# Moving the split activations by 32 bytes in SBUF, from 64 to 96 bytes off the weights modulo 128

## What is computed

```python
# first block
h = rmsnorm(x, norm1_g);  hp = h @ w_in           # 1024 -> 512 + 512 + 768 + 24 + 2048
y_ssm = s5_mixer(hp[..., :o1], ...)               # state-space mixer, ends in a 512x512 gate
y_nsa = nsa_mixer(hp[..., o1:o2], ...)            # sparse attention
merged = gate0 * (y_ssm @ w_proj_ssm) + gate1 * (y_nsa @ w_proj_nsa)
x = x + merged @ w_out
x = x + jnp.square(jax.nn.relu(rmsnorm(x) @ w_up)) @ w_down           # 1024 -> 4096 -> 1024
# second block, layers 0 (retention) and 1 (latent attention)
for l in range(2):
    x = x + 0.5 * rms_norm(swiglu(rms_norm(x), w_gu[l, 0], w_down[l, 0]))   # 1024 -> 2 x 2816 -> 1024
    tok, qm = retention_mixer(...) if l == 0 else mla_mixer(...)
    x = x + rms_norm(concat([tok, memory_attention(qm, mem_n, w_kv[l])]) @ w_o[l])
    x = x + 0.5 * rms_norm(swiglu(rms_norm(x), w_gu[l, 1], w_down[l, 1]))
```

## Time and profile before

| | us |
|---|---|
| median of 3 runs (1472.91 to 1474.15) | 1473.9 |
| span of the profiled execution | 1470.6 |
| TensorE matmul busy in it | 1401.7 |
| TensorE weight load busy in it | 1358.3 |
| VectorE busy | 922.4 |
| ScalarE busy | 732.0 |
| GpSimd busy | 192.7 |

### The profile page before, as it was taken

The page is one execution under the profiler, slowest core; times in us unless marked ns, Lnnn a source line. Parts: engine busy times, 40 slices in busy tenths (PEclk is TensorE's granted clock), DMA queues, the critical chain, the costliest instruction groups (busy, mean ns, idle before and its releaser), DMA issues.

```text
span 1470.6 us, 28247 instructions
## 1 busy us (share of the span) xinstructions
PE 1401.7 (95%) x11538; PEld 1358.3 (92%) x11538; DVE 922.4 (63%) x1368; ACT 732.0 (50%) x1205; POOL 192.7 (13%) x210
## 2 busy tenths in 40 slices
PE   5899899999999999999998999999999989899998
PEld 5878799999999999998898999999999987899998
DVE  7998786666535665556765665556564467565644
ACT  7712755544435454455446454455444364554443
POOL 0465000022000111013101111011110010111100
PEclk9899899999999999999999999999999989999999
DMA  9223324455554555544342555544555341345551
GB/s 372 105 103 116 127 86 174 159 204 185 194 185 160 177 195 191 195 173 155 135 144 99 190 197 189 198 172 172 188 198 199 146 170 58 109 178 195 192 200 58
DMA packets 36815, 244.33 MB, mean 166 GB/s; under 512 B 4208, under 2 KB 5360, under 8 KB 8816
## 3 DMA queue, kind: packets, MB, share of 16 engines
q1 hardware_dynamic: 34992, 238.17, 44.7%
q10 hardware_dynamic: 1728, 4.81, 0.9%
HBM read 241.67 MB, written 1.05 MB: 165 GB/s over the span
## 4 chain that ended last, share of the span: by engine, by line
PE 81%; DVE 9%; ACT 5%; issue 2%; POOL 2%; DMA 1%; SPq 0%; DVEq 0%; ACTq 0%; POOLq 0%
PE ps L1891 49%; PE ps L1931 26%; DVE wlo L1083 3%; PE ps L2114 1%; PE ps L2140 1%; ACT whi L592 1%; DVE alo L1478 1%; PE ps L2130 1%; DMA xtok<-in_xt 1%; POOL pr L1809 1%; POOL pr L1808 1%; PE ps L2019 1%; ACT junk L829 1%; DVE yr L1456 0%; ACT pP L782 0%
## 5 line engine op out<-in xcount | busy, mean ns | idle before, releaser
L1083 DVE TENSOR_TENSOR wlo<-raw,whi 128x1024 fp32r<-128x1024 f32 (+1 forms) x434 | 505.1, 1205 | 273.3 <-ACT whi L592 273.2
L1891 PE MATMUL ps<-ahi,whi 128*128 128x256 f32 x2112 | 599.5, 284 | 32.1 <-DVE wlo L1083 18.0
L592 ACT ACTIVATE whi<-raw 128x1024 fp32r<-128x1024 f32 (+1 forms) x434 | 427.2, 1032 | 368.8 <-PE ps L1931 188.1
L1891 PE MATMUL ps<-alo,whi 128*128 128x256 f32 x2112 | 595.4, 282 | 0.0
L1891 PE MATMUL ps<-ahi,wlo 128*128 128x256 f32 x2112 | 594.0, 281 | 0.0
L1891 PEld LDWEIGHTS ps<-ahi,whi 128*128 128x128 f32 x2112 | 403.1, 191 | 38.2 <-issue 23.5
L1891 PEld LDWEIGHTS ps<-alo,whi 128*128 128x128 f32 x2112 | 402.8, 191 | 0.7 <-issue 0.7
L1891 PEld LDWEIGHTS ps<-ahi,wlo 128*128 128x128 f32 x2112 | 401.9, 190 | 0.0
L1829 POOL TENSOR_TENSOR hlo<-fh,hhi 128x256 f32 (+3 forms) x104 | 86.1, 828 | 756.2 <-ACT hhi L899 545.5
L1538 DVE TENSOR_TENSOR fa<-ps,r 128x512 f32<-128x512 f32 x104 | 71.9, 692 | 171.1 <-PE ps L1891 170.9
L1931 PE MATMUL ps<-whi,hhi 128*128 128x256 f32 x960 | 149.1, 277 | 0.0
(11 more groups left out here) (350 smaller groups left out, 1362.9 us busy)
## 6 DMA issues: line engine op xcount, KB each, us to landing
raw<-in_w_gu SPq DMA_DIRECT2D x88, 1024.0 KB, 4.8
raw<-in_w_fd SPq DMA_DIRECT2D x44, 1024.0 KB, 4.8
raw<-in_w_up SPq DMA_DIRECT2D x16, 1024.0 KB, 4.8
raw<-in_w_dn SPq DMA_DIRECT2D x16, 1024.0 KB, 4.8
raw<-in_w_ret SPq DMA_DIRECT2D x13, 1024.0 KB, 4.8
raw<-in_w_mg SPq DMA_DIRECT2D x8, 1024.0 KB, 4.9
raw<-in_w_o SPq DMA_DIRECT2D x8, 1024.0 KB, 6.3
raw<-in_w_mem SPq DMA_DIRECT2D x4, 1024.0 KB, 4.7
```

Source lines behind the costliest of these rows:

```text
L592: nc.scalar.activation(whi[:, m % SPL, c], raw[:, n % RAW, c], ACT.Copy).then_inc(S("w_hi"), 1)
L1083: ins = tt(wlo[:, m % SPL, c], raw[:, n % RAW, c], whi[:, m % SPL, c].bitcast(F32), ALU.subtract)
L1891: ins = mm(dst, lhsT, rhs, start=k == 0 and p == 0, stop=k == kt - 1 and p == len(pairs) - 1)
```

## The change

Three lines in the layout, none in the work: the instructions of all five engines, their order and their waits are the same.

```diff
@@ -279,10 +279,12 @@
         at_warm = [base[0] + 32]
         half_q = sb("half_q", [P, 1])
         warm = sb("warm", [P, 1], where=at_warm)
+        base[0] += 32
         at_ahi = [base[0]]
         ahi = sb("ahi", [P, KT, T], F32R)
         at_alo = [base[0]]
         alo = sb("alo", [P, KT, T], F32R)
+        base[0] += -base[0] % 64
         st = sb("st", [P, TT, 8])
         at_yT = [base[0]]
         yT = sb("yT", [P, KT, T])
@@ -382,7 +384,7 @@
         end_nsa = w[0]
 
         w = [phase]
-        w[0] += (64 - w[0]) % 128
+        w[0] += (96 - w[0]) % 128
         hhi = sb("hhi", [P, FF1_T, T], F32R, where=w)
         hlo = sb("hlo", [P, FF1_T, T], F32R, where=w)
         fa = sb("fa", [P, 2, 2 * T], where=w)
```

## The result

| | before | after |
|---|---|---|
| median, us | 1473.9 (1472.91 to 1474.15) | 1499.4 (1492.97, 1499.41, 1499.73) |
| ratio, 95% interval | | 1.0153 (1.0128 to 1.0178) |
| profiled execution: span, us | 1470.6 | 1491.2 |
| granted clock, mean | 0.982 | 0.987 |

The kernel became 1.5% slower, 25.5 us in the medians. The profiled execution of after is its fastest run. Its granted clock is higher, too: (1 - 0.982) x 1470.6 = 26.5 us of full-speed time were lost to the lower level before, (1 - 0.987) x 1491.2 = 19.4 us after. So the difference of the spans, 20.6 us, would be about 27.7 at an equal clock. This is an estimate: it takes TensorE to be at work while the clock is low, and the mean clock is known to 0.0005 only, 0.7 us each.

What follows compares the result with a forecast made beforehand. Bound taken as TensorE's matmul intervals, 1401.7 of 1470.6 us busy. Terms 3.0 + 9.2 + 0.8 + 1.1 - 1.0 = +13.1 us gave span 1483.7, median 1487.0; forecast's own range 1479 to 1499, 8 in 10 1436 to 1512.

Steps and rivals of the forecast that it cites:

- Gate and up projections, "117.8 already, 0": Four gate and up projections, 1008 matmuls each: already at the 117.8 ns assumed for the new distances, so 0 us.
- Up projection +3.0: First feed-forward's up projection, 720 matmuls: 84.8 in place of 81.8 us, +3.0 us.
- Four later down projections +9.2: Four later down projections, 528 matmuls each: 62.2 in place of 59.9 us, +2.3 each, +9.2 us.
- First down projection 0: First feed-forward's down projection, 768 matmuls: already at 117.8 ns, so 0 us.
- Single units +1.1, layer 1's output projection +0.8: Five single units rising from 5.44 to 5.66 us, +1.1; layer 1's mixer output projection, 192 matmuls from 113.8 ns, +0.8.
- `mhi` pairs -1.0: 432 matmuls with `mhi`/`mlo` and the `y` pairs go from distance 0 to 64, from 120.0 to 117.8 ns: -1.0 us.
- Everything else 0: Residual transposes, half a microsecond at most, and other engines' writes starting at multiples of 32, covered by matmuls: 0 us.
- From span to median +3.3: Whole runs: their median lies 3.3 us above the profiled span, so 1483.7 becomes 1487.0 us.
- 96 parts the readers: Rival, main streams: distance 96 parts weight load and stream; 1427 us at 111.7 ns, or 1444 at 113.4; chance 0.22.
- The sign matters: Rival: units at 96 good, downs at 32 bad, 1466 us, chance 0.14; the other way round, +12, counted with forecast.
- 32 and 96 are worse than 0: Rival, units and down projections: 120.0 ns everywhere gives +33 us, 1507; 123 ns gives 1537; chance 0.15.
- Nothing that counts: Rival: halfway value is 116.7 ns, 1476 us, or the address does not matter, 1474 us; chance 0.15 together.

Runs made afterwards that it cites:

- weights_back: Against the change, weights raw, whi, wlo moved to 96 modulo 128, everything behind them back on multiples of 64, distances unchanged: 1495.9 us.
- ahi96: Half of the change: against the kernel before, only ahi/alo moved to 96; hhi shifted along, putting down projections at distance 64: 1501.6 us.
- d32: Against the kernel before, activations placed 32 bytes past the weights modulo 256 (units at 32, down projections at 224): 1487.2 us.
- both32: Against the kernel before, activations placed 32 past the weights modulo 128, in fact units at 160 and down projections at 96 modulo 256: 1490.6 us.
- d0: Against the kernel before, activations at the same address as the weights modulo 256 (units and down projections at 0): 1505.2 us.
- d192: Against the kernel before, ahi/alo and hhi/hlo moved by 128 bytes, so units at 192 and down projections at 64: 1461.7 us.
- wide: Addresses of the kernel before; matmuls in down stream 512 columns per weight load in place of 256: 1481.1 us.
- roots5: Layout of the kernel before; a short product formed twice ahead of the units that follow, so the long stream starts at another moment: 1476.3 us.
- d192_wide0: Against the kernel before, units at 192 and down projections at 0 with 512-column matmuls, three rounds: median 1454.6 us, ratio 0.9877.

## Why the prediction was right or wrong

The direction held, and so did the idea that the distance between the operands sets the interval. The form that the prediction gave this idea did not: the distance doesn't count modulo 128, and the interval at 96 isn't halfway between those at 0 and 64. +13.1 us was forecast, +25.5 measured, and two terms make most of the difference.

- **Gate and up projections, "117.8 already, 0":** This is the step that failed. They take 120.0 ns: +2.2 us each, +8.9 in all. The prediction called itself wrong above 1 ns per matmul, and they moved by 2.2. The median, 1499.4, lies just past the 1479 to 1499 of the forecast itself; the wider range, 1436 to 1512, held it because 1507 had been counted as a rival. Underneath was "halfway between distance 0 and distance 64, since 32 and 96 both lie halfway". weights_back and ahi96 show that 96 has the ceiling, as 0 has; d32 shows 116.7 to 117.8 at 32. The ceiling itself, 120.0 "with nothing to forbid more", was not passed in any stretch by more than 0.3 ns.
- **Up projection +3.0:** +4.8, by the same term.
- **Four later down projections +9.2:** +8.3. The value for -96 was nearly right, 117.4 ns for 117.8, by luck: it is 160 and not 32.
- **First down projection 0:** +0.7 us (118.7 ns). weights_back has 117.3 ns in the same place at the same distance, so this place has two values at one distance, too.
- **Single units +1.1, layer 1's output projection +0.8:** the five units moved by 0.3 us each as forecast, but those at 5.66 moved by 0.1 as well. The remainder, 27.7 less 22.7, about 5 us at an equal clock and not known to better than 1 or 2 us, must lie in these and the units between the stretches; it was not parted further.
- **`mhi` pairs -1.0:** 117.9 ns for the 117.8 forecast.
- **Everything else 0:** right. weights_back takes the writes of the other engines out; `alo` at the transitions kept its 2.43 us.
- **From span to median +3.3:** the profiled runs lie 1.7 to 1.9 us above their spans. The rest of the 3.3 was the difference between one run and the median.

**The rivals.** "96 parts the readers" is out: 96 has the longest interval. "The sign matters" is right as a mechanism (both32), in the form the prediction wrote as "the other way round": units at 120.0, and its +12 was too low, as the downs did not fall to 113.4. "32 and 96 are worse than 0" came nearest in size, 1507, and is half right: 96 has the 120.0 ns of 0, and -96 does not. "Nothing that counts" is out. The rule of the Trainium skill ("SBUF — State Buffer", section "SBUF: two separate sides") that TensorE's ports never wait on anyone doesn't bear the reading that an address can't matter to TensorE; whether a port waits, no run shows. d0 and d192 hold the same instructions at other addresses; a gate and up projection takes 120.94 us in one and 114.25 in the other.

**What stays open.** That the load of the next weights and the stream collide was only inferred. wide refuted its simplest form, and no run shows the collision. Why one distance has two forms, and what chooses between them, is open as well: wide and roots5 changed it in streams whose instructions and addresses are as before, d192 shows both forms among four equal projections, and none of it was foretold. So part of what d192_wide0 wins could be lost by an edit elsewhere. A second profile of one kernel would show whether the form repeats. The distances of 16, 48 and 112 weren't tried, nor units with 512 columns.

One small reading of the prediction was off: the 128-column row gives (1.84 - 0.28) / 14 = 111.4 ns and not 112. No term of the forecast uses it.

## What to carry to other kernels

When TensorE is busy all the time and waits for nothing, divide a long stretch of the chain by its matmuls: if one shape shows several intervals, the placement of its operands may be a knob, here 1505 against 1462 us by placement alone (single runs of d0 and d192). Tabulate the distance moving minus stationary modulo 256 for each pair, and don't interpolate between two measured distances; a run with one tensor moved is cheap, and a price found for 256 columns doesn't hold for 512. Judge such a change by stretches at full clock, as whole runs of one kernel spread over 15 us.

## What the runs showed of the hardware that was not expected

- The interval of a matmul with 128 x 128 float32r weights and 256 columns depends on the distance between its operands, given here modulo 256. From the long gate and up and later down projections: 0: 120.0 ns, even; 32: 116.7 or 117.8; 64: 113.4 or 117.8; 80: 118.3 or 120.0; 96: 120.0; 128: 118.7; 160: 117.3; 176: 118.8; 192: 113.3 or 117.8; 224: 118.4.
- With 512 columns it is 226.9 ns at 0 and 233.3 at 192.
- A stream at 32, 64, 80 or 192 can run in one of two forms, in gate and up projections for over a hundred us. At 160 the first down projection has 117.3 ns in weights_back and 118.7 in after. Streams changed their form in runs whose edit was elsewhere (wide, roots5); whether the edit did it is not shown.
- The granted clock's mean varied from 0.977 to 0.987 between profiled runs. Of the seven executions of the kernel before that ran beside d192_wide0, the shortest, 1467.8 us, had 0.988 and the longest, 1483.0, had 0.977.
